# Gated recurrence in a two-block transformer kernel: cumulated decays made two rounds ahead, and the order of ScalarE and VectorE in a round

## The chip, the cores and the metric

The kernel runs on one core of a Trainium2 chip, as one launch. The metric is the device time of that launch in microseconds (us), the median of several runs. A profiled execution of the same program gives the rows shown below.

## The reference

The program computes two blocks one after the other, for one sequence of 256 positions and width 1024. The first block puts 16 meta tokens in front (272 positions), multiplies by one projection, and sends the parts to two mixers: a gated recurrence (HGRN2) with 8 heads of width 128, and a Mamba-2 mixer. Then come an output projection and a gated MLP with a short convolution. The second block has a retention mixer and 16 experts with expert choice. Only the HGRN2 mixer is touched by the change. Cut to what matters, per head:

```python
f = lb + (1.0 - lb) * sigmoid(f_pre)
k = 1.0 - f
log_f = log(f)
qa = silu(q)
bcum = cumsum(log_f)                       # restarted at every chunk of 16
q_dec, k_inv = q * exp(bcum), k * exp(-bcum)
k_end = k * exp(blast - bcum)
o = causal(q_dec @ k_inv.T) @ v + q_dec @ state
o = o * rsqrt(mean(o * o) + eps) * norm_w * silu(g)
```

`lb` is a vector with one number per channel, made from `hg_lb_logits`. The kernel uses the same recurrence at chunk lengths 16, 32, 64 and 128 (its four "levels").

## The kernel before, in words

All activations lie with channels on the partitions and the 272 positions along the row. The projection of the first block is made as 52 output tiles of 128 channels, numbered j = 0 to 51, in the order of `ORDER`. TensorE (PE) makes a tile with 8 products in fp32 (L872), in one of three PSUM banks that it uses in turn, so a tile can be opened only when the tile three before it has been copied out. ScalarE (ACT) copies each tile out (`evict`, L1254), with Silu, Sigmoid or a plain copy according to the block of columns. Every engine runs its instructions in the order in which they are written; the three loops `for j in range(NPROJ)`, one for each engine, set that order by hand, with semaphores between them.

From j = 32 on, the work of the HGRN2 heads is laid between the tiles, three steps (`hgrn(j)`) for one head h, so one round of a head takes three tiles:

- **Step 0.** PE `hg_turn(h)`: transposes of values and decayed keys (L793, L795), which wait for `hg_staged`; scores of the four levels (L802); then it waits for `hg_v` and makes the last small scores (L804), waits for `hg_ke` and makes the two states (L808). Then the tile j. ACT `hg_keys(h)` (L1373) copies the turned keys, `hg_log_mean(h-1)` takes Ln of the mean square of the head before (L1365), `hg_log(h+1)` takes Ln of the gate (L1351), `hg_inverse(h-1)` is an Exp (L1369), a Square of the output follows (L1390), then `hg_exps(h+1)` (L1356 to L1358), and only then the tile's copy. VectorE (DVE) has `hg_values(h)` (L1845, L1846; it signals `hg_v`), `hg_mask(h)` (L1853), `hg_states(h)` (L1860) and `hg_cumulate(h+1)`: gate (L1817), key (L1819), after `hg_log` four scans (L1822) and four differences (L1826).
- **Step 1.** PE `hg_out(h)` (L815 to L818) and tile j+1. DVE `hg_gate(h)` (L1867), `hg_finish(h-1)` (L1872), `hg_decay(h+1)` (L1835 to L1840; it signals `hg_staged`).
- **Step 2.** PE `hg_mean(h)` (L826) and tile j+2. For ACT only the tile's copy, for DVE nothing, apart from the last head.

Head 0 is prepared at j = 30. The heads' last steps fall behind the tiles, between the first products of the output projection (L890). At j = 48 and 49 a pass of the other mixer's gate lies in the same queues: DVE `m2_gate(0)` (L1800) and ACT `gate_squares(0)` (L1400). Before an activation whose function isn't in the loaded table, ACT has a table load, which the compiler puts in. Lines that say this best:

```python
pe.wait_ge(ev("hg_v"), h + 1)
pe.matmul(ps[0:16, 6, 384:400], hg_K0[:, b, 256:T], hg_B[:, b, 0, 256:T], start=True, stop=True).then_inc(ev("hg_scores"), 1)
...
evict(f"p{j}", proj[:, 4 * unit_ + m, :], T, fn)
```

Of the kernel before, what the change touches and what calls it, by code (L numbers as in the profile page):

```python
# [19 lines left out]
ACT = mybir.ActivationFunctionType  # L20
# [130 lines left out]
def build(nc, a, out):  # L151
    with ExitStack() as ctx:
# [106 lines left out]

        hg_f, hg_k, hg_lf, hg_sq = (proj[:, TBM + i, :] for i in range(4))  # L260

# [986 lines left out]
        def _(act):  # L1248
# [100 lines left out]
            def hg_log(h):  # L1349
                act.wait_ge(ev("hg_f"), h + 1)  # L1350
                act.activation(hg_lf, hg_f, ACT.Ln).then_inc(ev("hg_log"), 1)  # L1351

# [22 lines left out]
            def hgrn(j):  # L1375
# [3 lines left out]
                if (j - 32) % 3 == 0:  # L1379
                    hg_keys(h)  # L1380
                    if h:
                        hg_log_mean(h - 1)
                    if h + 1 < HEADS:
                        hg_log(h + 1)
                    if h:
# [4 lines left out]
                    act.activation(hg_sq, ps[:, 6, 0:T], ACT.Square).then_inc(ev("hg_squared"), 1)  # L1390
                    if h + 1 < HEADS:
                        hg_exps(h + 1)
                if (j - 32) % 3 == 2 and h == HEADS - 1:
                    hg_log_mean(h)
                    hg_inverse(h)

# [206 lines left out]
        def _(dve):  # L1603
# [33 lines left out]
            lb, oml = small[:, 96:104], small[:, 104:112]  # L1637
            st.link(tt(lb, small[:, 0:8], small[:, 24:32], ALU.mult))
            st.link(ts(oml, lb, -1.0, 1.0, ALU.mult, ALU.add))

# [173 lines left out]
            def hg_cumulate(h):  # L1814
                b = h % 2
                dve.wait_ge(ev("proj_tiles"), 16 if h < 4 else 32)
                st.link(ts(hg_f, proj[:, h + TF_, :], oml[:, h:h + 1], lb[:, h:h + 1], ALU.mult, ALU.add))  # L1817
                dve.nop().then_inc(ev("hg_f"), 1)
                st(ts(hg_k, hg_f, -1.0, 1.0, ALU.mult, ALU.add))  # L1819
                dve.wait_ge(ev("hg_log"), h + 1)  # L1820
# [53 lines left out]
            def hgrn(j):  # L1874
# [3 lines left out]
                if (j - 32) % 3 == 0:  # L1878
                    hg_values(h)
                    hg_mask(h)  # L1880
                    hg_states(h)
                    if h == 0:
                        mod_add(1)
                    if h + 1 < HEADS:
                        hg_cumulate(h + 1)
                if (j - 32) % 3 == 1:
                    hg_gate(h)
                    if h:
                        hg_finish(h - 1)
                    if h + 1 < HEADS:  # L1890
                        hg_decay(h + 1)
                if (j - 32) % 3 == 2 and h == HEADS - 1:
# [389 lines left out]
```

## Time and profile before

| | us |
|---|---|
| median of 3 runs (lowest, highest) | 1702.42 (1701.29, 1703.94) |
| the profiled execution, its own time | 1704.49 |
| its span, first to last instruction | 1702.7 |
| PE busy (share of the span) | 1349.4 (79%) |
| DVE busy | 507.1 (30%) |
| ACT busy | 450.4 (26%) |
| GpSimd busy | 232.8 (14%) |

The difference between a profiled execution's own time and its span lies around the program. A row of the timeline has start, duration, engine, line and operation, and in brackets how long the engine sat idle before it and what released it; "DVEq" is VectorE's own sequencer, which signals without an instruction that computes. PEld is TensorE's weight load, which runs beside its products. A line is that of the kernel before.

### The profile page before, as it was taken

To read this page: it belongs to the slowest core of one execution; us is meant where nothing else is said; L and a number is where in the kernel's file an instruction comes from. 1 tells how busy PE (TensorE), PEld (TensorE's weight loads), DVE (VectorE), ACT (ScalarE), POOL (GpSimd) and SP (SyncE) were. 2 spreads that over 40 slices of the span, in tenths; PEclk is the share of its full clock that TensorE was granted. 3 is DMA by queue.
4 is the path that set the end of the run, shared out by engine and by line. 5 is a ranking of instruction groups with operands and counts; after the bars stand their busy time and mean duration, and the time that the engine had idled before them with its cause. 6 is when DMAs were issued, how large, how long until landed. Compare 5 with 4: busy or idle time off the path is not lost.

```text
span 1702.7 us, 21054 instructions
## 1 busy us (share of the span) xinstructions
PE 1349.4 (79%) x8581; PEld 831.1 (49%) x8581; DVE 507.1 (30%) x919; ACT 450.4 (26%) x675; POOL 232.8 (14%) x100
## 2 busy tenths in 40 slices
PE   6989999999999999988767577666657667666665
PEld 4877788879998988944222122112212221221221
DVE  3874677436568455622000000000000000000001
ACT  4853465436564533721000000000000000000001
POOL 0000000028767654400000000000000000000000
PEclk9999999999999999997887878888887877987887
DMA  7936322168534552285999999999999999999995
GB/s 242 361 149 235 112 99 100 50 210 273 186 137 181 201 188 99 100 357 212 428 429 428 429 428 429 428 428 429 429 429 428 429 429 428 429 428 429 428 428 250
DMA packets 92335, 524.01 MB, mean 308 GB/s; under 512 B 8009, under 2 KB 30945, under 8 KB 64369
## 3 DMA queue, kind: packets, MB, share of 16 engines
q1 hardware_dynamic: 92057, 523.08, 75.4%
q8 instruction: 44, 0.72, 0.2%
q14 instruction: 18, 0.15, 0.0%
q10 hardware_dynamic: 216, 0.06, 0.0%
HBM read 522.08 MB, written 1.05 MB: 307 GB/s over the span
## 4 chain that ended last, share of the span: by engine, by line
DMA 47%; PE 38%; DVE 8%; ACT 3%; issue 1%; SPq 1%; POOL 0%; ACTq 0%; DVEq 0%
DMA ring<-in_w_down 23%; DMA ring<-in_w_up 23%; PE ps L657 6%; PE ps L661 6%; PE ps L658 6%; PE ps L1213 3%; PE ps L890 3%; PE ps L1226 3%; PE ps L872 2%; PE ps L1123 2%; PE ps L641 1%; SPq L502 1%; DVE arena L2024 1%; PE ps L802 1%; PE ps L706 1%
## 5 line engine op out<-in xcount | busy, mean ns | idle before, releaser
L1213 PE MATMUL ps<-ring,arena 128*32 128x512 f32 x1984 | 297.5, 745 | 163.2 <-DMA ring<-in_w_up 136.0
L1599 POOL TENSOR_TENSOR ring_r<-ring,ring_r 128x1024 fp32r<-128x1024 f32 (+1 forms) x96 | 232.6, 2441 | 483.3 <-ACT ring_r L1265 483.3
L657 PE MATMUL ps<-arena_r,ring_r 128*128 128x258 f32 (+3 forms) x960 | 289.3, 301 | 9.7 <-PE ps L661 3.4
L661 PE MATMUL ps<-arena_r,ring_r 128*128 128x258 f32 (+3 forms) x960 | 281.4, 293 | 0.0
L1226 PE MATMUL ps<-ring,arena 128*32 128x512 f32 x1024 | 171.2, 804 | 104.1 <-DMA ring<-in_w_down 97.1
L1213 PEld LDWEIGHTS ps<-ring,arena 128*32 128x32 f32 x1984 | 65.0, 127 | 378.3 <-DMA ring<-in_w_up 204.7
L657 PEld LDWEIGHTS ps<-arena_r,ring_r 128*128 128x128 f32 x960 | 183.2, 191 | 20.6 <-issue 13.2
L661 PEld LDWEIGHTS ps<-arena_r,ring_r 128*128 128x128 f32 x960 | 182.4, 190 | 2.9
L658 PE MATMUL ps<-arena_r,ring_r 128*128 128x256 f32 (+2 forms) x608 | 180.8, 297 | 0.0
L2239 DVE TENSOR_TENSOR arena<-arena,ps 128x512 f32<-128x512 f32 x16 | 11.0, 688 | 448.7 <-PE ps L1213 448.7
L1226 PEld LDWEIGHTS ps<-ring,arena 128*32 128x32 f32 x1024 | 33.0, 129 | 225.1 <-DMA ring<-in_w_down 147.6
L1265 ACT ACTIVATE ring_r<-ring 128x1024 fp32r<-128x1024 f32 (+1 forms) x122 | 126.0, 1037 | 42.9 <-PE ps L658 23.0
L658 PEld LDWEIGHTS ps<-arena_r,ring_r 128*128 128x128 f32 x608 | 116.3, 191 | 4.0 <-issue 1.0
L872 PE MATMUL ps<-uT,ring 128*128 128x272 f32 x416 | 100.2, 395 | 3.2 <-DVE uT L1643 3.2
L658 PE MATMUL ps<-uT_r,ring_r 128*128 128x258 f32 x352 | 99.5, 283 | 0.0
L2241 DVE COPY arena<-ps 128x512 f32<-128x512 f32 x16 | 11.1, 692 | 290.7 <-PE ps L1226 290.7
L1569 ACT ACTIVATE arena<-ps 128x512 f32<-128x512 f32 x16 | 9.6, 597 | 316.1 <-PE ps L1218 316.1
L872 PEld LDWEIGHTS ps<-uT,ring 128*128 128x128 f32 x416 | 77.6, 190 | 18.5 <-issue 3.6
L1567 ACT ACTIVATE arena<-ps 128x512 f32<-128x512 f32 x16 | 9.6, 597 | 282.7 <-PE ps L1213 282.7
L1573 ACT ACTIVATE arena<-ps 128x512 f32<-128x512 f32 x16 | 9.6, 597 | 264.6 <-PE ps L1226 264.6
L1235 PE MATMUL ps<-arena 128*128 128x512 f32 x128 | 67.1, 672 | 14.2 <-DVEq L2248 13.5
L641 PEld LDWEIGHTS ps<-arena,hT 128*128 128x128 f32 x512 | 65.8, 205 | 8.9 <-issue 7.1
(370 smaller groups left out, 1478.1 us busy)
## 6 DMA issues: line engine op xcount, KB each, us to landing
ring<-in_w_gate SPq DMA_DIRECT2D x64, 2048.0 KB, 25.9
ring<-in_w_down SPq DMA_DIRECT2D x64, 2048.0 KB, 26.2
ring<-in_w_up SPq DMA_DIRECT2D x60, 2048.0 KB, 21.9
ring<-in_w_in SPq DMA_DIRECT2D x20, 2048.0 KB, 11.7
ring<-in_w_ada SPq DMA_DIRECT2D x12, 2048.0 KB, 8.5
ring<-in_ffn_w_up SPq DMA_DIRECT2D x22, 1024.0 KB, 7.9
ring<-in_w_out SPq DMA_DIRECT2D x6, 2048.0 KB, 8.0
ring<-in_ffn_w_down SPq DMA_DIRECT2D x4, 2048.0 KB, 8.4
```

The source lines that it names most:

```text
L641: mm = pe.matmul(o, l, r, start=i == 0, stop=i == len(pairs) - 1)
L657: pe.matmul(o, hi[:, k, :], r_(xhi(k0 + k)), start=first and k == 0, stop=False)
L658: mm = pe.matmul(o, hi[:, k, :], r_(xlo(k0 + k)), start=False, stop=False)
L661: mm = pe.matmul(o, lo[:, k, :], r_(xhi(k0 + k)), start=False, stop=last and k == nk - 1)
L872: mm = pe.matmul(o[:, 0:T], w[:, k, :], uT[:, k, :], start=k == 0, stop=k == KT - 1)
L890: mm = pe.matmul(o[:, 0:KEPT], kcols(u_out[cb][half], m)[:, i, :], x, start=first and n == 0, stop=last and n == len(blocks) - 1)
L1123: mm = pe.matmul(ps[:, 4 + 2 * w + cb, :], x[:, w * P:w * P + P], slot(u_out2[cb]).rearrange("p (k c) -> p k c", k=KT)[:, i, :], start=n = ...
L1213: mm = pe.matmul(ps[32 * j:32 * j + 32, half, :], xs[:, kt, :], wk[:, 512 * j:512 * j + 512], start=kt == 0, stop=kt == KT - 1)
L1226: mm = pe.matmul(ps[32 * j:32 * j + 32, half, :], heT[:, j, 32 * i:32 * i + 32], w[:, j, 512 * half:512 * half + 512], start=i == 0, stop= ...
L1235: mm = pe.matmul(ps[:, 4 + b, :], Gt[:, w * P:w * P + P], ye[:, half * 512:half * 512 + 512], start=first, stop=last, skip_group_check=True)
L1265: act.activation(r_(rounded(c)), chunks[c][1], ACT.Copy).then_inc(ev("w_hi"), 1)
L1599: pool.tensor_tensor(r_(w), w, f_(rounded(c)), ALU.subtract).then_inc(ev("w_lo"), 1)
```

## The change

The gate itself is no longer stored. ACT takes the logarithm straight from the sigmoid, Ln(oml * sigmoid + lb) with one scale and one bias per channel, and DVE makes the key in one instruction, (lb - 1) * sigmoid + (1 - lb), for which one small vector `noml` is made once. `hg_log` now waits for `hg_b` of the head before, or, for head 0, for the other mixer's last output. In the rounds, head 1 is prepared as before, in round 0. From head 2 on, `hg_cumulate(h+2)` stands in step 2 of round h on DVE, `hg_exps(h+1)` in step 0 of round h on ACT ahead of the Square, and `hg_decay(h+1)` in step 0 of round h on DVE, behind `hg_states(h)`. `hg_log_mean(h)` moves from step 0 of round h+1 to step 2 of round h, and `hg_log(h+2)` stands behind it.

```diff
--- before.py
+++ after.py
@@ -257,7 +257,7 @@
         hg_S = A.take(2, P)
         hg_inv = A.take(1, T)[:, 0]
 
-        hg_f, hg_k, hg_lf, hg_sq = (proj[:, TBM + i, :] for i in range(4))
+        hg_k, hg_lf, hg_sq = (proj[:, TBM + i, :] for i in range(1, 4))
 
         A = Arena(x_at)
         m2_t = A.take(2, T)
@@ -1347,8 +1347,12 @@
                     act.activation(buf, buf, ACT.Exp).then_inc(ev("m2_seg_exp"), 1)
 
             def hg_log(h):
-                act.wait_ge(ev("hg_f"), h + 1)
-                act.activation(hg_lf, hg_f, ACT.Ln).then_inc(ev("hg_log"), 1)
+                if h:
+                    act.wait_ge(ev("hg_b"), h)
+                else:
+                    act.wait_ge(ev("m2_out"), 8)
+                lb, oml = small[:, 96 + h:97 + h], small[:, 104 + h:105 + h]
+                act.activation(hg_lf, proj[:, h + TF_, :], ACT.Ln, scale=oml, bias=lb).then_inc(ev("hg_log"), 1)
 
             def hg_exps(h):
                 b = h % 2
@@ -1378,21 +1382,24 @@
                     return
                 if (j - 32) % 3 == 0:
                     hg_keys(h)
-                    if h:
-                        hg_log_mean(h - 1)
-                    if h + 1 < HEADS:
-                        hg_log(h + 1)
+                    if h == 0:
+                        hg_log(1)
+                    elif h + 1 < HEADS:
+                        hg_exps(h + 1)
                     if h:
                         hg_inverse(h - 1)
                     act.wait_ge(ev("hg_out"), h + 1)
                     if h:
                         act.wait_ge(ev("hg_mean"), h)
                     act.activation(hg_sq, ps[:, 6, 0:T], ACT.Square).then_inc(ev("hg_squared"), 1)
-                    if h + 1 < HEADS:
-                        hg_exps(h + 1)
-                if (j - 32) % 3 == 2 and h == HEADS - 1:
+                    if h == 0:
+                        hg_exps(1)
+                if (j - 32) % 3 == 2:
                     hg_log_mean(h)
-                    hg_inverse(h)
+                    if h + 2 < HEADS:
+                        hg_log(h + 2)
+                    if h == HEADS - 1:
+                        hg_inverse(h)
 
             def gate_squares(g):
                 act.wait_ge(ev("m2_gated"), g + 1)
@@ -1636,6 +1643,8 @@
             st.link(dve.reciprocal(small[:, 24:32], small[:, 16:24]))
             lb, oml = small[:, 96:104], small[:, 104:112]
             st.link(tt(lb, small[:, 0:8], small[:, 24:32], ALU.mult))
+            noml = small[:, 112:120]
+            st(ts(noml, lb, -1.0, None, ALU.add))
             st.link(ts(oml, lb, -1.0, 1.0, ALU.mult, ALU.add))
 
             def scaled(name, k, t0):
@@ -1814,9 +1823,7 @@
             def hg_cumulate(h):
                 b = h % 2
                 dve.wait_ge(ev("proj_tiles"), 16 if h < 4 else 32)
-                st.link(ts(hg_f, proj[:, h + TF_, :], oml[:, h:h + 1], lb[:, h:h + 1], ALU.mult, ALU.add))
-                dve.nop().then_inc(ev("hg_f"), 1)
-                st(ts(hg_k, hg_f, -1.0, 1.0, ALU.mult, ALU.add))
+                st(ts(hg_k, proj[:, h + TF_, :], noml[:, h:h + 1], oml[:, h:h + 1], ALU.mult, ALU.add))
                 dve.wait_ge(ev("hg_log"), h + 1)
                 for l in range(4):
                     st(dve.tensor_tensor_scan(hg_B[:, b, l, :], reset[:, l, :], hg_lf, 0.0, ALU.mult, ALU.add))
@@ -1881,14 +1888,18 @@
                     hg_states(h)
                     if h == 0:
                         mod_add(1)
-                    if h + 1 < HEADS:
-                        hg_cumulate(h + 1)
+                    if h == 0:
+                        hg_cumulate(1)
+                    elif h + 1 < HEADS:
+                        hg_decay(h + 1)
                 if (j - 32) % 3 == 1:
                     hg_gate(h)
                     if h:
                         hg_finish(h - 1)
-                    if h + 1 < HEADS:
-                        hg_decay(h + 1)
+                    else:
+                        hg_decay(1)
+                if (j - 32) % 3 == 2 and h + 2 < HEADS:
+                    hg_cumulate(h + 2)
                 if (j - 32) % 3 == 2 and h == HEADS - 1:
                     hg_finish(h)
```

PE's instructions and their order are the same in both. On ACT, one round of head 2 before, from the keys' copy to the copy of the first tile (the names in it: `s_tiles_freed` and `s_tiles_done` are the PSUM tiles, the others the events named above):

```order
L1373 ACTIVATE arena<-ps 128x256 [waits s_tiles_freed,s_hg_turned]
L1365 ACT_TABLE_LOAD [waits s_hg_head]
L1365 ACTIVATE arena<-ps,eps 128x272 [waits s_hg_mean]
L1351 ACTIVATE arena<-arena 128x272 [waits s_hg_f]
L1369 ACT_TABLE_LOAD
L1369 ACTIVATE arena<-arena 128x272 [waits s_hg_log_mean]
L1390 ACTIVATE arena<-ps 128x272 [waits s_hg_mean,s_hg_out]
L1356 ACTIVATE arena<-arena 128x272 [waits s_hg_b]
L1357 ACTIVATE arena<-arena 128x1024
L1358 ACTIVATE arena<-arena 128x1088 [waits s_act_steps]
L1254 ACTIVATE arena<-ps 128x272 [waits s_tiles_done]
```

Both logarithms stand here between two copies of tiles, in step 0. The round of head 2 in the changed kernel, whose lines are numbered otherwise: L1377 is the keys' copy, L1360 to L1362 the exponentials, L1373 the inverse, L1394 the Square, L1369 the logarithm of the mean, L1355 that of the gate.

```order
L1377 ACTIVATE arena<-ps 128x256 [waits s_tiles_freed,s_hg_turned]
L1360 ACT_TABLE_LOAD
L1360 ACTIVATE arena<-arena 128x272 [waits s_hg_b]
...
L1362 ACTIVATE arena<-arena 128x1088 [waits s_act_steps]
L1373 ACTIVATE arena<-arena 128x272 [waits s_hg_log_mean]
L1394 ACTIVATE arena<-ps 128x272 [waits s_hg_mean,s_hg_out]
...
L1254 ACTIVATE arena<-ps 128x272 [waits s_tiles_freed,s_tiles_done]
L1369 ACT_TABLE_LOAD [waits s_tiles_freed,s_hg_head]
L1369 ACTIVATE arena<-ps,eps 128x272 [waits s_hg_mean]
L1355 ACTIVATE arena<-arena,small 128x272 [waits s_hg_b]
L1254 ACT_TABLE_LOAD
L1254 ACTIVATE arena<-ps 128x272 [waits s_tiles_done]
```

The logarithms and their table load now stand behind the copy of tile j+1, ahead of the copy of tile j+2. On DVE, before, from the finish of one round to the values of the next:

```order
L1872 TENSOR_TENSOR arena<-arena 128x272 [waits s_hg_gated,s_hg_inverse]
L1835 COPY small<-arena 128x1 [waits s_hg_exp]
L1836 TENSOR_TENSOR arena<-arena 128x272
L1837 TENSOR_TENSOR arena<-arena 128x1024
L1840 TENSOR_TENSOR arena<-arena 128x1088 [waits s_proj_tiles,s_dve_steps]
L1845 COPY arena<-ps 128x256 [waits s_dve_steps,s_hg_turned]
L1846 COPY arena<-ps 16x128
```

The same stretch in the changed kernel (L1879 is the finish, L1826 the key, L1829 the scans, L1833 the differences, L1852 and L1853 the values):

```order
L1879 TENSOR_TENSOR arena<-arena 128x272 [waits s_hg_gated,s_hg_inverse]
L1826 TENSOR_SCALAR arena<-arena,small 128x272 [waits s_proj_tiles]
L1829 SCALAR_TENSOR_TENSOR arena<-cst,arena 128x272 [waits s_hg_log]
...
L1833 TENSOR_TENSOR arena<-arena 128x256 [waits s_dve_steps]
...
L1852 COPY arena<-ps 128x256 [waits s_dve_steps,s_hg_turned]
L1853 COPY arena<-ps 16x128
```

The products of `hg_decay` have left this place for the one behind the states, and the scans and differences of the head after next have taken it.

## Rows read from the trace of the kernel before

**Rows 1.** The page: the span, and the chain that ended last by engine.
```profile
span 1702.7 us, 21054 instructions
...
DMA 47%; PE 38%; DVE 8%; ACT 3%; issue 1%; SPq 1%; POOL 0%; ACTq 0%; DVEq 0%
```

**Rows 2.** Waits, 170 to 320 us: total us, times, the longest.
```profile
ACT arena L1351 <- DVEq L1818: 25.4, 8, 6.6
...
PE ps L793 <- DVEq L1841: 3.3, 4, 2.1
...
PE ps L808 <- ACT arena L1373: 1.0, 1, 1.0
```

**Rows 3.** Timeline of PE, 223 to 257 us: a round of head 3.
```profile
239.94 0.49 PE L793 MATMUL ps<-cst,arena 128*128 128x128 f32 x3
...
242.37 0.21 PE L804 MATMUL ps<-arena 128*16 128x16 f32 x2
...
243.06 3.83 PE L872 MATMUL ps<-uT,ring 128*128 128x272 f32 x16
...
248.06 3.91 PE L872 MATMUL ps<-uT,ring 128*128 128x272 f32 x16
251.81 0.62 PE L826 MATMUL ps<-arena,ones 128*128 128x272 f32 x2
...
256.40 0.52 PE L793 MATMUL ps<-cst,arena 128*128 128x128 f32 x3 [0.30 <-DVEq L1841]
```

**Rows 4.** Timeline of DVE, 220 to 245 us.
```profile
230.00 2.57 DVE L1822 TENSOR_TENSOR_SCAN arena<-cst,arena 128x272 f32<-128x272 f32 x4
232.61 1.43 DVE L1826 TENSOR_TENSOR arena<-arena 128x256 f32<-128x256 f32 x4
234.27 0.50 DVE L1867 SCALAR_TENSOR_TENSOR arena<-ps,par,arena 128x272 f32<-128x272 f32 x1 [0.22 <-DVE arena L1826]
...
240.69 0.42 DVE L1845 COPY arena<-ps 128x256 f32<-128x256 f32 x1 [1.04 <-PE ps L795]
241.03 0.27 DVE L1846 COPY arena<-ps 16x128 f32<-16x128 f32 x1
```

**Rows 5.** Timeline of ACT, 220 to 245 us.
```profile
224.56 1.28 ACT L1365 ACT_TABLE_LOAD   x1
225.85 0.49 ACT L1365 ACTIVATE arena<-ps,eps 128x272 f32<-128x272 f32 x1
...
240.14 0.40 ACT L1254 ACTIVATE arena<-ps 128x272 f32<-128x272 f32 x1 [1.31 <-PE ps L872]
```

**Rows 6.** Line L1430, an activation with scale and bias per channel.
```profile
L1430 ACT ACTIVATE arena<-arena,par x12: 612/616/618, 31.0 to 70.4; 128x272 f32<-128x272 f32 x12
```

**Rows 7.** Timeline of all engines, 160 to 215 us: from round 0 into round 1.
```profile
196.23 0.41 DVE L1817 TENSOR_SCALAR arena<-arena,small 128x272 f32<-128x272 f32 x1
...
197.20 2.57 DVE L1822 TENSOR_TENSOR_SCAN arena<-cst,arena 128x272 f32<-128x272 f32 x4
...
202.73 1.11 ACT L1358 ACTIVATE arena<-arena 128x1088 f32<-128x1088 f32 x1
...
205.16 0.91 ACT L1254 ACTIVATE arena<-ps 128x272 f32<-128x272 f32 x2
...
206.95 0.55 PE L793 MATMUL ps<-cst,arena 128*128 128x128 f32 x3 [0.65 <-DVEq L1841]
...
209.43 0.21 PE L804 MATMUL ps<-arena 128*16 128x16 f32 x2
```

**Rows 8.** The same view: the turn of head 0 and the tile behind it.
```profile
187.67 0.55 PE L793 MATMUL ps<-cst,arena 128*128 128x128 f32 x3 [2.12 <-DVEq L1841]
...
192.38 2.92 PE L872 MATMUL ps<-uT,ring 128*128 128x272 f32 x12
```

**Rows 9.** Busy time by engine and granted clock (PEclk) in two stretches.
```profile
core 0: us, PE busy (x) PEld busy (x) DVE busy (x) ACT busy (x) POOL busy (x), PEclk, DMA share, GB/s
...
190.00:192.00 2.00, 2.00 (x11) 1.74 (x10) 0.23 (x1) 0.16 (x1) 0.00 (x0) 0.50 1.05 396
291.00:293.00 2.00, 1.04 (x10) 0.82 (x9) 1.11 (x4) 1.86 (x7) 0.00 (x0) 1.00 0.00 0
```

## The prediction

> **What bounds the kernel now.** I read the page first, for the chain that ended last: transfers hold 47% of it, and PE 38% [rows 1]. The transfers belong to the experts at the end; the stage that the change touches, about 176 to 330 us, lies ahead of them, and there the chain runs through PE with pieces of DVE and ACT. What this stage loses or gains moves everything behind it, because the later weight loads are released by PE's progress. I therefore count a microsecond here as a microsecond at the end.
>
> The waits of the stage come next [rows 2]. ACT sits 25.4 us in front of Ln of the gate, but an idle ACT costs nothing by itself. What counts is PE: it waits 3.3 us in total for `hg_staged` (DVE, L1841), 2.1 of them in front of head 0, and once 1.0 us for the keys' copy. The timeline shows how little that leaves: the turns of heads 3 and 4 start at 239.94 and 256.40, a round of 16.46 us with 0.30 of waiting [rows 3]. PE is nearly full, so a shorter chain can give back only these few waits, while a longer chain costs in every round. The question is where the new order puts its longest chain against PE's round.
>
> **The change, part by part.**
>
> *The gate in one ScalarE instruction.* For heads 0 and 1 nothing is moved, only the gate's DVE instruction no longer stands ahead of ACT's Ln. Before, the gate starts at 196.23 and the scans at 197.20, 0.97 us [rows 7]. Now Ln runs long before, and DVE needs only the key with two operands per channel, 0.41 us like the gate's row. So the scans start 0.55 us earlier, for head 0 and for head 1. Both times PE was waiting for `hg_staged` (2.12 us [rows 8] and 0.65 us [rows 7]), so both are gained, unless the DVE of round 0 is held by another wait: 0.55 each, 0 to 0.6 as bounds. In the later rounds the key's row is off the path. The Ln itself gets dearer: with scale and bias per channel I take 0.62 us from L1430 [rows 6] for the 0.49 or less of a logarithm without the scale [rows 5]. The one `noml` instruction on 8 columns is under 0.1 us and I count it as nothing; it hides beside the table loads and products of the start.
>
> *The moved products of `hg_decay`.* They now run behind the states of round h, for head h+1, about 8 us ahead of the next turn. PE's waits for `hg_staged` go from round 1 on: 3.3 less the 2.1 of head 0 is 1.2 us at most. In the forecast this gain isn't added, because the next part takes its place.
>
> *The cumulated decays, now behind the mean.* This is the term that decides. In step 2 of round h the chain is: PE ends tile j+1 and makes the mean; ACT copies tile j+1, loads the Ln table, takes both logarithms; DVE scans and subtracts for head h+2; and only then DVE may run `hg_values(h+1)`, for which PE waits in front of L804. Step by step, from the end of tile j+1: copy 0.43 with its start [rows 5]; semaphore 0.1; table load 1.28 [rows 5]; Ln 0.49 and Ln 0.62, overlapping a little, 1.04; semaphore 0.05; scans and differences until DVE is free, 230.00 to 234.27, 4.27 [rows 4]; values, 240.69 to 241.30, 0.61 [rows 4]; signal to PE 0.13. That is 7.91 us. The other half of the circle is PE's: from L804 at 242.37 over tile, output and the next tile to its end at 248.06 + 3.91 = 251.97, 9.60 us [rows 3]. The round becomes 7.91 + 9.60 = 17.5 us instead of 16.46, so 1.05 us more in each. The mean isn't the late one: it starts at 251.81 and ends at 252.43 [rows 3], and the table load now stands behind the copy anyway.
>
> *The first such chain is longer.* `hg_exps(1)` still comes at the end of ACT's step 0 in round 0, so its last row ends at 202.73 + 1.11 = 203.84 [rows 7], 203.29 with the 0.55 gained. Then follow a table load for the tiles' function 1.28, two copies 0.91 [rows 7], the Ln table 1.28, both Ln 1.04, scans and differences 4.27, values and signal 0.74, small steps 0.17: L804 of head 1 at 213.0 instead of 209.43 [rows 7]. That is +3.55 us, with both early gains already in it. PE starts the turn at about 206.35 and then stands some 4 us in front of L804.
>
> *From head 1 to head 6* there are five rounds with a `hg_cumulate(h+2)` in them: 5 x 1.05 = +5.3 us. In round 6 PE loses 1.0 us before, in front of L808 [rows 2], because the keys' copy stood behind the squares of the other mixer; in the new order DVE's `m2_gate(0)` runs ahead of the scans and the squares end before the copy is wanted: -1.0. Rounds 6 and 7 have no scans, and the steps behind the tiles keep their slack.
>
> *ACT's table loads.* There are four more over the whole program. Those in the rounds' chain are counted above, the others lie where ACT waits for a tile. The Trainium skill (ScalarE: Activation LUTs, Table sets: the hidden batching unit) speaks against such a change: activations should be batched by set. The same page (What ACT_TABLE_LOAD costs) puts a switch at about 2.66 us, the load of 1283 ns and a drain of about 1380 ns; by that the seven loads in my chains would be some 9.7 us dearer, a total near +19. The trace doesn't agree with the drain: the load at 224.56 lasts 1.28 us and the Ln starts at 225.85, 0.01 us later [rows 5].
>
> *PE's clock.* After the 2.12 us wait of head 0 the granted clock falls to 0.50, that is 1.2 of 2.4 GHz [rows 9], and from the turn to the tile PE takes 4.71 us (187.67 to 192.38 [rows 8]) against 3.12 (239.94 to 243.06 [rows 3]): 1.6 us more. After the stall of 1.0 us in round 6 it stays at 1.00 [rows 9]. A stall of 4 us is nearer to the first, so I take +1.6 once, for head 1. The stalls of about 1.3 us in the five later rounds lie between the two rows: 0 to 1.6 us each, and I take 0.
>
> **Sum.** +3.55 + 5.3 - 1.0 + 1.6 = +9.4 us. The rows come from an execution of 1704.49 us (span 1702.7), 2.1 above the median of the runs, 1702.42. The difference is the same whichever it is added to; added to the median it gives **1711.8 us**, and a profile of the changed kernel should have a span near 1712.
>
> **The rivals.**
>
> 1. *The same wait without the clock.* PE's stall of 4 us comes behind the transposes and scores and the clock stays up, or the fall of head 0 goes with its shorter wait (1.6 instead of 2.1 us). Then 1702.4 + 7.8 = 1710.2. For it speaks that 1.0 us costs no clock, against it the 2.1 us that did. If both falls are missing it is 1708.6.
> 2. *The clock falls again and again.* Each stall of 1.3 us lies in the part of the round where PE has small products. Two falls more give 1715.0, five 1719.8.
> 3. *Faster: the scans fit in front of the turn.* If PE isn't held at L804, only the gains stay: 0.55 twice, up to 1.2 of the later waits, 1.0 in round 6, together 3.3: 1699.1. The point from which this decides is the chain of 7.91 us: PE alone comes from the end of tile j+1 back to L804 in about 6.5 us (mean, tile, turn up to L804: 251.97 to 258.5), so the chain would have to be 1.4 us shorter, and in round 0 nearly 4. Durations of rows don't leave that open; it would need a mistake of mine in the order.
> 4. *Nothing measurable.* The stalls come as said, but half as long, since the order of ACT or the start of the scans is better than I think: between -3.4 and +3.4 us, which is also about what a measurement of this kernel can tell from no change (0.2%).
>
> **How the numbers follow.** Forecast with one fall of the clock at head 1: 0.43; rival 1: 0.25; rival 2: 0.20; rival 3: 0.04; rival 4: 0.08. The first three are all slower by more than 0.2% (above 1705.8): 0.88; within 0.2%: rival 4 and a half of rival 3: 0.09 with rounding; faster by over 0.2%: 0.03, as even the full gain of rival 3 only just reaches it. The range takes in rival 1 with both falls missing and an error of 0.25 us in each of six chains at the low end (1708.6 - 1.5 = 1707), and two to three falls more at the high end (1717): 1707 to 1717.
>
> **What would show it.** In the profile of the changed kernel PE must have a wait in front of the last small scores (L804) in heads 1 to 6, released by the values of DVE: some 4 us at head 1, 1.1 to 1.5 at the others; the wait at L808 in round 6 gone; turns of heads 3 and 4 some 17.5 us apart; `hg_staged` no longer waited for except at head 0, where the wait is 1.6 us. ACT's wait for Ln of the gate (25.4 us) should vanish, with no profit. The granted clock behind head 1's stall shows the last term. I am wrong if DVE's values start on time in round 2, if PE's round stays at 16.4 us, or if the difference at the end of the stage is made up later in front of the experts.

## The result, and the profile after

The changed kernel takes 1715.44 us in the median of 5 runs (1711.17 to 1718.82) against 1702.42 before (also 5 runs, 1701.29 to 1703.94); the ratio is 1.0075, with an interval of 1.0056 to 1.0093. It is slower, by about 13 us in the medians; a ratio and its interval come from all runs of both kernels, and can lie some 0.1% off the ratio of the two medians. The forecast was 1711.8, with a range of 1707 to 1717. The profiled execution of the change took 1715.44 us with a span of 1713.7; the one of before had a span of 1702.7, so the two traces differ by 11.0 us, and it is these 11.0 that can be followed row by row. The other 2 us are that the profiled execution of before lay 2.1 us above its median. One execution in the whole study, of split_signal below, came out at 2989.7 us with a granted clock of 0.44, and no median or ratio has it in.

The page of the changed kernel, its first and fourth part, against [rows 1]:

```profile
span 1713.7 us, 21043 instructions
...
DMA 47%; PE 37%; DVE 9%; ACT 4%; issue 1%; SPq 1%; POOL 0%; ACTq 0%; DVEq 0%
```

PE's share of the chain has fallen by a point, and those of DVE and of ACT have each risen by one. The waits of the stage (170 to 330 us; engine, line <- releaser: total us, times, the longest) say where:

```profile
ACT arena L1394 <- PE ps L818: 36.2, 8, 6.9
DVE arena L1829 <- ACT arena L1355: 23.6, 6, 5.0
...
PE ps L804 <- DVEq L1855: 9.6, 6, 3.9
...
PE ps L793 <- DVEq L1848: 1.5, 1, 1.5
```

In [rows 2] ACT stood 25.4 us in front of the gate's logarithm. That wait has gone, and ACT stands 36.2 us in front of its squares instead: no profit. PE has lost its wait in front of L808 (1.0) and all waits for `hg_staged` (L793) but the one of head 0. In their place stands a new one, 9.6 us in front of the last small scores, L804, once in each of heads 1 to 6, released by DVE's values (now L1852, L1853). PE's timeline shows them (start, us, engine, line, in brackets the wait and its releaser):

```profile
187.06 0.55 PE L793 MATMUL ps<-cst,arena 128*128 128x128 f32 x3 [1.48 <-DVEq L1848]
...
189.54 0.21 PE L804 MATMUL ps<-arena 128*16 128x16 f32 x2
...
210.59 0.24 PE L804 MATMUL ps<-arena 128*16 128x16 f32 x2 [3.88 <-DVEq L1855]
...
217.98 0.46 PE L815 MATMUL ps<-arena 128*128 128x128 f32 x2
...
231.11 0.21 PE L804 MATMUL ps<-arena 128*16 128x16 f32 x2 [1.35 <-DVEq L1855]
...
248.52 0.21 PE L804 MATMUL ps<-arena 128*16 128x16 f32 x2 [0.81 <-DVEq L1855]
...
301.15 0.21 PE L804 MATMUL ps<-arena 128*16 128x16 f32 x2 [1.35 <-DVEq L1855]
...
318.64 0.49 PE L793 MATMUL ps<-cst,arena 128*128 128x128 f32 x3
```

From head 2 to head 3 PE needs 248.52 - 231.11 = 17.41 us; the round of [rows 3] took 16.5. The chain that holds it is on ACT and DVE. It is shown here where it ends in PE's L804 of head 2, at 231.11:

```profile
223.34 0.40 ACT L1254 ACTIVATE arena<-ps 128x272 f32<-128x272 f32 x1 [1.66 <-PE ps L872]
223.89 1.28 ACT L1369 ACT_TABLE_LOAD   x1 [0.16 <-ACT arena L1254]
225.19 0.49 ACT L1369 ACTIVATE arena<-ps,eps 128x272 f32<-128x272 f32 x1
225.57 0.60 ACT L1355 ACTIVATE arena<-arena,small 128x272 f32<-128x272 f32 x1
```

```profile
226.21 2.57 DVE L1829 TENSOR_TENSOR_SCAN arena<-cst,arena 128x272 f32<-128x272 f32 x4 [4.98 <-ACT arena L1355]
228.81 1.43 DVE L1833 TENSOR_TENSOR arena<-arena 128x256 f32<-128x256 f32 x4
230.39 0.42 DVE L1852 COPY arena<-ps 128x256 f32<-128x256 f32 x1
230.73 0.27 DVE L1853 COPY arena<-ps 16x128 f32<-16x128 f32 x1
```

Copy of tile, load of Ln's table, Ln of the mean (L1369), Ln of the gate (L1355), scans, differences, and only then the values for which PE waits: 223.34 to 231.11, 7.77 us. One round later it runs from 240.75 to 248.52, 7.77 us again. DVE itself stood idle for 4.98 us in front of the scans, with the values that PE wanted queued behind them.

Where the 11.0 us are, from the first start of a line in each trace:

| from, to | before | after | difference |
|---|---|---|---|
| start of the span to the turn of head 0 (L793) | 187.7 | 187.1 | -0.6 |
| turn of head 0 to the first L890 | 117.3 | 126.4 | +9.1 |
| first L890 to the first L940 | 63.5 | 63.5 | 0.0 |
| first L940 to the experts' first L1213 | 418.3 | 422.0 | +3.7 |
| L1213 to the end | 916.0 | 914.8 | -1.2 |

### The profile page after: what moved, and what is told of

Same layout as the page of the kernel before. It is cut to its first block, busy times and chain, and to the rows that moved or that the text cites. A ratio compares the mean times of both kernels' runs of the same rounds, so it can differ in the third digit from the quotient of the medians.

```text
span 1713.7 us, 21043 instructions
## 1 busy us (share of the span) xinstructions
PE 1351.8 (79%) x8581; PEld 831.5 (49%) x8581; DVE 509.6 (30%) x912; ACT 455.5 (27%) x679; POOL 232.2 (14%) x100
## 3 DMA queue, kind: packets, MB, share of 16 engines
HBM read 522.08 MB, written 1.05 MB: 305 GB/s over the span
## 4 chain that ended last, share of the span: by engine, by line
DMA 47%; PE 37%; DVE 9%; ACT 4%; issue 1%; SPq 1%; POOL 0%; ACTq 0%; DVEq 0%
DMA ring<-in_w_down 23%; DMA ring<-in_w_up 23%; PE ps L657 6%; PE ps L661 5%; PE ps L658 5%; PE ps L1213 3%; PE ps L872 3%; PE ps L890 3%; PE ps L1226 3%; PE ps L1123 2%; PE ps L641 1%; DVE arena L1829 1%; DVE arena L2035 1%; SPq L502 1%; DMA ring<-in_w_in 1%
## 5 line engine op out<-in xcount | busy, mean ns | idle before, releaser
L1213 PE MATMUL ps<-ring,arena 128*32 128x512 f32 x1984 | 297.8, 746 | 162.9 <-DMA ring<-in_w_up 135.2
L657 PE MATMUL ps<-arena_r,ring_r 128*128 128x258 f32 (+3 forms) x960 | 289.7, 302 | 10.6 <-PE ps L661 3.3
L1213 PEld LDWEIGHTS ps<-ring,arena 128*32 128x32 f32 x1984 | 65.1, 127 | 377.9 <-DMA ring<-in_w_up 204.8
L657 PEld LDWEIGHTS ps<-arena_r,ring_r 128*128 128x128 f32 x960 | 183.5, 191 | 21.7 <-issue 13.0
L1265 ACT ACTIVATE ring_r<-ring 128x1024 fp32r<-128x1024 f32 (+1 forms) x122 | 126.0, 1037 | 42.9 <-PE ps L658 23.0
L1235 PE MATMUL ps<-arena 128*128 128x512 f32 x128 | 65.1, 656 | 14.2 <-DVEq L2259 13.5
```

The costliest lines, as they stand in the source:

```text
L657: pe.matmul(o, hi[:, k, :], r_(xhi(k0 + k)), start=first and k == 0, stop=False)
L1213: mm = pe.matmul(ps[32 * j:32 * j + 32, half, :], xs[:, kt, :], wk[:, 512 * j:512 * j + 512], start=kt == 0, stop=kt == KT - 1)
L1235: mm = pe.matmul(ps[:, 4 + b, :], Gt[:, w * P:w * P + P], ye[:, half * 512:half * 512 + 512], start=first, stop=last, skip_group_check=True)
L1265: act.activation(r_(rounded(c)), chunks[c][1], ACT.Copy).then_inc(ev("w_hi"), 1)
```

## The experiments

Where nothing else is said, an experiment stands against the kernel before, run on the same chip: 1703.36 us in the median of 23 runs for gate_alone, log_ahead, ln_doubled and fill_scores, 1702.60 of 18 for the other four. Single runs scatter by up to some 8 to 10 us (the kernel before 1701.51 to 1709.64, gate_alone 1698.27 to 1708.37), so I take medians of a few runs as good to one or two; the stage itself (turn of head 0 to the first L890) repeats much better, 126.4 and 126.0 us in two traces of the change. I therefore read the stage first and the total second.

My theory was that of the prediction: the round is closed by the chain through the Ln of the next-but-one head, 5 x 1.05 us; the first such chain costs PE a stand of 4 us, and the clock falls behind it. Against it stood three others: that the gate's part costs something; that what counts is not the chain but the new place of the scans or of the products; and that the stage isn't what moves the end.

**gate_alone: the gate's part without the new order.** The kernel before with these hunks of the change alone (and the one that makes `noml`):

```diff
-                act.wait_ge(ev("hg_f"), h + 1)
-                act.activation(hg_lf, hg_f, ACT.Ln).then_inc(ev("hg_log"), 1)
+                if h:
+                    act.wait_ge(ev("hg_b"), h)
+                else:
+                    act.wait_ge(ev("m2_out"), 8)
+                lb, oml = small[:, 96 + h:97 + h], small[:, 104 + h:105 + h]
+                act.activation(hg_lf, proj[:, h + TF_, :], ACT.Ln, scale=oml, bias=lb).then_inc(ev("hg_log"), 1)
...
-                st.link(ts(hg_f, proj[:, h + TF_, :], oml[:, h:h + 1], lb[:, h:h + 1], ALU.mult, ALU.add))
-                dve.nop().then_inc(ev("hg_f"), 1)
-                st(ts(hg_k, hg_f, -1.0, 1.0, ALU.mult, ALU.add))
+                st(ts(hg_k, proj[:, h + TF_, :], noml[:, h:h + 1], oml[:, h:h + 1], ALU.mult, ALU.add))
```

> The kernel before with the gate's part of the change alone: Ln straight from the sigmoid with scale and bias, one instruction for the key, all places in the rounds as before. Theory: the scans of heads 0 and 1 start 0.55 us earlier and PE waits that much less in front of both turns, and, as in the trace of the change, the clock may stay at 1.00 behind the turn of head 0, worth 1.6 us: 1.1 to 2.7 us under the kernel before, 1699.7 to 1701.3; in the other rounds up to 1.2 us more of waits for hg_staged vanish. Rival: the loss of the change lies in the dearer Ln (0.60 us instead of 0.43): then this kernel is slower than before by 0.17 us a head, 1.4 us.

Measured: 1701.36 us (1698.27 to 1708.37, 12 runs), ratio 0.9989 (0.9974 to 1.0005). The median is 2.0 us under that of the kernel before, though the interval of the ratio still takes in 1. The stage takes 114.0 us, 3.2 less than before. PE's waits in it that answer to [rows 2]:

```profile
PE ps L793 <- DVEq L1845: 1.5, 1, 1.5
...
PE ps L808 <- ACT arena L1377: 0.3, 1, 0.3
```

The 3.3 us of waits for `hg_staged` have become 1.5, all in front of head 0, and the one for the keys' copy 0.3 instead of 1.0. The 3.2 us add up: 1.2 of waits behind head 0, 0.7 at the keys, and 1.3 of clock behind the turn of head 0 (2.48 us from L793 to L804 instead of 3.82). So the gate's part alone already removes every wait that the products' new place was to remove: after it the order had only the 0.3 us at the keys left to gain in this stage. The rival that the dearer Ln of the gate's part makes the loss (+1.4 us, a ratio of 1.0008) is out.

**order_only: the new order without the gate's part.** The changed kernel with the old `hg_log` and the old gate and key in `hg_cumulate`, the hunks above turned round.

> The changed kernel's order with the gate as before: gate and key in two DVE instructions, Ln without scale and bias. Theory: the whole loss is in the order. The chain in front of L804 is 0.17 us shorter a round (Ln 0.43 instead of 0.60), six rounds -1.0 us; the scans of heads 0 and 1 start 0.55 us later, +1.1, and the clock may fall at head 0 as in the kernel before, +1.6: 0 to 1.7 us over the change, 1715.4 to 1717. PE waits in front of L804 at heads 1 to 6. Rival (the dear Ln with scale and bias makes the loss): back near the kernel before.

Measured: 1716.67 us (1713.58 to 1719.6, 6 runs), ratio 1.0070 (1.0055 to 1.0086); stage 127.4 us. Its waits:

```profile
PE ps L804 <- DVEq L1851: 8.5, 6, 3.7
...
PE ps L793 <- DVEq L1844: 2.8, 2, 2.1
```

The whole loss is the order's. The waits at L804 are 3.70, 1.17, 0.63, 0.68, 1.18 and 1.17 us, each 0.17 to 0.19 under those of the change, and the old Ln without scale takes 0.42 us on average, the new one 0.60: the same 0.18. So the dearer Ln of the gate's part, which costs nothing in the old order, is on the path in the new one. The turn of head 0 has its 2.1 us wait back. The total is 1.0 us over the change on the same chip (1715.64, change_again2 below), inside the 0 to 1.7 that were expected.

**log_ahead: the logarithm out of step 2.** The change, but ACT makes the gate's Ln of head h+2 in step 0 of the round, where the Ln's operand is long there:

```diff
                     elif h + 1 < HEADS:
+                        if h + 2 < HEADS:
+                            hg_log(h + 2)
                         hg_exps(h + 1)
...
                     if h == 0:
                         hg_exps(1)
+                        hg_log(2)
...
                     hg_log_mean(h)
-                    if h + 2 < HEADS:
-                        hg_log(h + 2)
```

> The changed kernel with hg_log(h+2) moved out of step 2 into step 0 of round h (in front of the exponentials; in round 0 behind them), so DVE's scans don't wait for ACT. Theory (the chain copy, Ln table, two Ln, scans, differences, values holds PE in front of L804): the waits of PE in front of L804 at heads 2 to 6 (5.7 us together in the change) are gone, though ACT has more table loads, 82 in all instead of 77; at head 1 DVE itself comes late, because hg_decay(1) ends just ahead of the turn and the scans and differences take 4.1 us: a wait of about 2.7 us stays there instead of 3.9. So 6.9 us under the change, about 1708.5, and up to 3 us less again if the clock doesn't fall at head 1. Rival (table loads on ACT, or DVE's own load, make the loss): no gain, or slower than the change by 5 x 1.28 us.

Measured: 1708.3 us (1704.63 to 1711.73, 12 runs), ratio 1.0024 (1.0013 to 1.0035); stage 117.8 us against 126.4. It comes within 0.2 us of what was expected, and in the place that was expected:

```profile
209.61 0.24 PE L804 MATMUL ps<-arena 128*16 128x16 f32 x2 [2.72 <-DVEq L1856]
...
215.73 0.46 PE L815 MATMUL ps<-arena 128*128 128x128 f32 x2
...
227.43 0.22 PE L804 MATMUL ps<-arena 128*16 128x16 f32 x2
```

Only the wait of head 1 is left, 2.72 us; from head 2 on PE never stands at L804 and the rounds are back at 16.0 to 16.5 us. The scans still stand in step 2 and the products behind the states, so from head 2 on neither of these two moves costs by itself: what closed the round was the Ln behind the mean. At head 1 it is otherwise. The Ln is there in time, and DVE is late all the same, because the scans of head 2 stand between the products for head 1 and the values. With the clock behind it (6.12 us from L804 to L815, 4.68 before) this stand is what keeps the stage 3.8 us above the 114.0 of gate_alone. So of the 12.3 us that the new order costs the stage, 8.5 go with the place of the Ln; the other 3.8 the trace puts down to the place of the scans ahead of head 1's values, which no run took away by itself.

**ln_doubled: the suspected link made dearer.** The change with the gate's Ln of step 2 made twice in six rounds.

```diff
                     if h + 2 < HEADS:
+                        lb, oml = small[:, 98 + h:99 + h], small[:, 106 + h:107 + h]
+                        act.wait_ge(ev("hg_b"), h + 2)
+                        st.link(act.activation(hg_lf, proj[:, h + 2 + TF_, :], ACT.Ln, scale=oml, bias=lb))
                         hg_log(h + 2)
```

> The changed kernel with Ln of the gate done twice over for heads 2 to 7, the second behind the first (0.60 us and some 0.1 us of semaphore each). Theory: this lies in the chain that holds PE, so each of six rounds is 0.7 us longer: 4.2 us over the change, about 1719.6, and PE's waits in front of L804 are that much longer. Rival (the chain is hidden, PE or the clock sets the rounds): no difference.

Measured: 1720.31 us (1718.72 to 1727.51, 5 runs), ratio 1.0090 (1.0070 to 1.0110).

```profile
PE ps L804 <- DVEq L1858: 13.5, 6, 4.5
```

Six more logarithms of 0.6 us add 13.5 - 9.6 = 3.9 us of PE's waits, 0.65 each: the Ln is on the path in all six heads, one for one. The stage grew by 8.7 us and not by 3.9, because in this trace the granted clock fell in three later rounds too; in 238 to 242 us its mean was 0.57. They are the rounds of heads 2, 5 and 6, where PE now stands 2.00 us and L804 to L815 takes 6.0 to 6.3 us instead of 4.4 to 4.7; behind the stands of 1.46 and 1.51 us of heads 3 and 4 it takes 4.37 as ever. The profiled execution was the highest of five (1727.51) and began the stage 4.9 us late; the median lies nearer to the expectation, 1719.6. Whether the other runs had these falls of the clock, no trace shows.

**fill_scores: is it the clock behind head 1?** The change with the scores of head 1 (L802) made three times, so that PE works in the time in which it would stand.

```diff
-                for l in range(4):
+                for l in list(range(4)) * (3 if h == 1 else 1):
```

> The changed kernel in which PE repeats the scores of head 1 twice more, 3.7 us of the 3.9 us that it stands in front of L804 there, with the same results. Theory (the clock falls because PE stands): the granted clock stays at 1.00 behind it, the stretch from L804 to the output's first product, 7.4 us in the change, goes to 4.4 us, so 3.0 us under the change, about 1712.4. Rival (the clock's fall has another cause, or the products cost more than the stall hides): no gain.

Measured: 1719.02 us (1713.7 to 1720.72, 6 runs), ratio 1.0078 (1.0058 to 1.0099). The total is a miss: I had forecast 1712.4. In the stage it did what was expected:

```profile
209.60 5.52 PE L802 MATMUL ps<-arena 128*128 128x128 f32 x48
215.44 0.21 PE L804 MATMUL ps<-arena 128*16 128x16 f32 x2 [0.31 <-DVEq L1855]
...
220.12 0.46 PE L815 MATMUL ps<-arena 128*128 128x128 f32 x2
```

Stretches around L804 of head 1, while PE would stand and behind it, first of this experiment, then of the change (us, then busy us and count of PE, PEld, DVE, ACT, POOL, then granted clock, DMA share, GB/s):

```profile
212.00:214.00 2.00, 2.00 (x20) 2.00 (x20) 1.97 (x5) 1.87 (x3) 0.00 (x0) 1.00 0.00 0
...
216.00:218.00 2.00, 2.00 (x12) 1.69 (x11) 1.83 (x6) 1.47 (x3) 0.00 (x0) 1.00 0.00 0
```

```profile
208.00:210.00 2.00, 0.00 (x0) 0.00 (x0) 1.82 (x6) 1.35 (x2) 0.00 (x0) 0.86 0.00 0
...
212.00:214.00 2.00, 2.00 (x5) 1.47 (x5) 1.72 (x7) 0.66 (x2) 0.00 (x0) 0.50 0.00 0
214.00:216.00 2.00, 2.00 (x6) 1.49 (x5) 1.97 (x3) 0.00 (x0) 0.00 (x0) 0.50 0.00 0
```

With PE kept at work the clock stays at 1.00 (2.4 GHz) and from L804 to L815 it takes 220.12 - 215.44 = 4.68 us; in the change it falls to 0.50 (1.2 GHz) while PE stands, stays there until a little after 216 us, and the same work takes 217.98 - 210.59 = 7.39, which is 2.7 more. The stage becomes 123.7 us, 2.7 less. Its profiled execution began the stage 4.8 us later (turn of head 0 at 191.90) and took 423.8 us from L940 to the experts; the six runs lie at 1713.7 to 1713.8 (two) and 1718.8 to 1720.7 (four). The slower four lie about as far above the other two as this late start is long, so the miss may sit ahead of the stage; no trace of one of the two shows it. That the clock behind head 1 costs 2.7 us of the stage is shown. That the end gets them back is not.

**change_again2: the change once more,** unaltered, to see what of its trace repeats.

> The changed kernel once more, beside the others on the same chip. Theory: PE's waits in front of L804 come again to 0.1 us (3.9 us at head 1, 0.8 to 1.4 at heads 2 to 6), so the first product of the output projection starts 8 to 9 us later than before. Behind that stretch the first profile of the change was 3.8 us longer up to the experts (418.3 against 422.0 us). If that belongs to the change, it is there again; if it is chance, this profile shows another value between 418 and 424.

Measured: 1715.64 us (1713.67 to 1718.84, 6 runs), ratio 1.0071 (1.0055 to 1.0087); the waits at L804 are again 3.88, 1.35, 0.81, 0.86, 1.35 and 1.36, and L940 to L1213 again 422.0. So the 3.7 us behind the stage were no accident of one execution.

**split_signal: a better kernel?** gate_alone, with ACT's signal for the decay products in two: K0 and D may be multiplied while ACT still makes its last exponential.

```diff
                 st.link(act.activation(hg_D[:, b], hg_D[:, b], ACT.Exp))
+                act.nop().then_inc(ev("hg_exp_d"), 1)
...
-                dve.wait_ge(ev("hg_exp"), h + 1)
-                st(dve.tensor_copy(small[:, 120 + b:121 + b], hg_B[:, b, 3, 255:256]))
+                dve.wait_ge(ev("hg_exp_d"), h + 1)
                 st(tt(hg_K0[:, b], hg_K0[:, b], hg_k, ALU.mult))
...
+                dve.wait_ge(ev("hg_exp"), h + 1)
+                st(dve.tensor_copy(small[:, 120 + b:121 + b], hg_B[:, b, 3, 255:256]))
```

> gate_alone with the exponentials' signal in two: DVE starts the products of keys and decays when ACT has made those two, while ACT still makes the third exponential (1.1 us). Theory: only the wait of PE for hg_staged at head 0 (1.5 us there) is on the path, so it shrinks by 1.0 us and nothing else moves: 1.0 us under gate_alone, about 1700.4. Rival: the semaphore of one more signal on ACT eats it: no difference.

Measured: 1702.49 us in the median of 11 runs (1698.04 to 1704.09), ratio 0.9989 (0.9978 to 1.0000). The total is a miss: about 1700.4 was expected, 1.0 under gate_alone, and the ratio is the same as that of gate_alone. PE's wait before head 0 is down from 1.48 to 0.38 us as meant:

```profile
PE ps L793 <- DVEq L1846: 0.4, 1, 0.4
```

The stage, 113.4 us, is the shortest of all, 0.7 under gate_alone, but its profiled execution took 422.0 us from L940 to the experts, like the change, although it has the old order. Together with gate_alone it suggests that the gate's half of the change is worth some 2 us in 1700 (0.9989 twice), at the limit of what can be measured. No version of this study beats the kernel before by more.

**busy_longer: does a microsecond of the stage reach the end?** gate_alone with the scores of heads 2 to 6 made twice: PE is busy and never stands. If later work absorbed what the stage loses, it would show here.

```diff
-                for l in range(4):
+                for l in list(range(4)) * (2 if 2 <= h <= 6 else 1):
```

> gate_alone in which PE repeats the scores of heads 2 to 6 once, with the same results: 5 x 1.9 us more of busy PE and no standing. Theory A (a microsecond of this stretch is one at the end, and only that): 9.4 us over gate_alone, about 1710.8, no fall of the clock in the rounds, and the stretch from there to the experts as long as in gate_alone (419 us). Theory B (a shift alone also lengthens what comes later, by where POOL and DVE then meet): that stretch is some 2 to 4 us longer, as it was in the four kernels with the new order, and the total 1713 to 1715.

Measured: 1710.94 us (1708.1 to 1715.76, 7 runs), ratio 1.0044 (1.0028 to 1.0061). That is 9.6 us over gate_alone, with 8.5 more in the stage (122.5 against 114.0), and theory A had 9.4. What the stage loses comes out at the end, all of it as nearly as these medians tell. From L940 to the experts it took 420.5 us against 419.1 in gate_alone. That lies between the two theories; the clock accounts for it (below).

**What the 3.7 us between L940 and the experts are.** They arise at two places, and both are of one kind: a DVE operation and one of GpSimd become ready almost together. At the first, DVE's row of the change, then GpSimd's:

```profile
473.30 2.62 DVE L1986 TENSOR_TENSOR arena_r<-arena,arena_r 128x256 fp32r<-128x256 f32 x1
```

```profile
473.05 5.10 POOL L1606 TENSOR_TENSOR ring_r<-ring,ring_r 128x1024 fp32r<-128x1024 f32 x2 [4.26 <-ACT ring_r L1265]
```

The same two in the kernel before:

```profile
464.87 0.42 DVE L1975 TENSOR_TENSOR arena_r<-arena,arena_r 128x256 fp32r<-128x256 f32 x1
```

```profile
464.97 4.94 POOL L1599 TENSOR_TENSOR ring_r<-ring,ring_r 128x1024 fp32r<-128x1024 f32 x2 [4.46 <-ACT ring_r L1265]
```

Before, DVE is 0.10 us ahead and takes 0.42 us; after, GpSimd is 0.25 us ahead and DVE takes 2.62. DVE stays late from there, and a product soon behind it (L657 at 479.20) waits 1.50 us for DVE, where the kernel before has no wait. From L940 to the last L986 behind this place it is 110.45 us before and 112.52 after, +2.1. GpSimd is first here in eight of the ten traces of this study, gate_alone, split_signal and busy_longer among them; only before and order_only have DVE first. At the second place, the change first:

```profile
724.00 2.81 DVE L2098 TENSOR_TENSOR arena<-arena,cst 128x512 f32<-128x512 f32 x1
```

```profile
723.87 2.39 POOL L1606 TENSOR_TENSOR ring_r<-ring,ring_r 128x1024 fp32r<-128x1024 f32 x1 [0.70 <-ACT ring_r L1265]
```

```profile
728.34 1.06 PE L1091 MATMUL ps<-cst,hT 128*128 128x128 f32 x8 [1.89 <-DVEq L2106]
```

The same three in the kernel before:

```profile
713.35 0.69 DVE L2087 TENSOR_TENSOR arena<-arena,cst 128x512 f32<-128x512 f32 x1
```

```profile
713.51 2.79 POOL L1599 TENSOR_TENSOR ring_r<-ring,ring_r 128x1024 fp32r<-128x1024 f32 x1 [0.98 <-ACT ring_r L1265]
```

```profile
715.92 1.03 PE L1091 MATMUL ps<-cst,hT 128*128 128x128 f32 x8
```

Before, DVE is 0.16 us ahead, takes 0.69 us, and PE doesn't wait. After, GpSimd is 0.13 us ahead, DVE takes 2.81 us, until 0.55 us behind GpSimd's end, and PE stands 1.89 us. All ten traces fall in line: with before, gate_alone and busy_longer DVE starts first, by 0.16 us each time, and takes 0.69; with the seven others GpSimd starts first, by 0.11 to 0.14 us, and DVE takes 2.80 to 2.82. From L940 to this L1091 it is 347.47 us before and 351.42 after, so both meetings together make +3.95, and what is left up to the experts is -0.2. The Trainium skill (SBUF — State Buffer, SBUF: two separate sides) says that a DVE operation with two inputs in SBUF and a GpSimd one that reads SBUF share a pair of ports under an exclusive lock, which the one that starts first keeps for its whole instruction. The ten traces agree with it at both places. Split_signal has the order of before and both meetings as in the change, so it isn't the new order as such that turns them round; between before and the change the two engines' starts moved against each other by 0.35 us at the first and 0.29 at the second. That a shift alone turns them round was not tried by itself.

Between the two meetings lies one more step of this size, in which the change and the kernel before agree. PE stands 1.80 to 1.84 us there for GpSimd in all ten traces; in seven of them, before and change too, the granted clock then falls to 0.50, and in gate_alone, log_ahead and ln_doubled it stays at 1.00. The stretch is 1.4 us shorter in these three. The change behind its stand of 1.81 us, then gate_alone behind its stand of 1.84 (columns as above; the granted clock is the third from the end):

```profile
560.00:565.00 5.00, 5.00 (x32) 5.00 (x31) 4.62 (x2) 1.63 (x2) 5.00 (x3) 0.66 0.99 401
```

```profile
548.00:553.00 5.00, 5.00 (x45) 5.00 (x44) 4.55 (x2) 1.55 (x2) 5.00 (x3) 1.00 0.99 397
```

That is why gate_alone, with the first meeting as in the change, still took only 419.1 us, and busy_longer 1.4 more.

## Why the prediction was right, and where it wasn't

The sign, the place and the mechanism were as predicted: PE waits at L804 in heads 1 to 6 for DVE's values, the wait at L808 is gone, `hg_staged` is waited for before head 0 alone, ACT's 25.4 us have gone without profit. Rivals 3 and 4 are out. (Rival 3's gains of 3.3 were too high in themselves: the 0.65 us wait of head 1 is in the second 0.55 and again in the 1.2.) That the measured 1715.44 lies in the range owes something to luck: the range reached up to 1717 for falls of the clock that did not come, and what filled it was not in the prediction (below). Term by term:

- **The rounds, 5 x 1.05.** Right. Chain 7.91 us forecast from the end of the tile; 7.82 measured (219.38 + 3.91 = 223.29 to 231.11). The three small gaps in it, 0.1, 0.05 and 0.13, for which the prediction has no row, are 0.15, 0.04 and 0.11 here. The rounds from head 2 to head 6 are 17.41, 17.42, 17.41 and 17.80 us against 17.5. The Ln with scale and bias takes 0.60 us where I took 0.62 from [rows 6]. From L804 of head 1 to that of head 6 it is 90.56 us, before 82.22 (209.43 to 291.65): +8.34. Of this 2.7 to 3.0 is the clock (below); 5.3 to 5.6 is left for five rounds. log_ahead shows that it is this chain, by taking it away.
- **Head 1, +3.55.** The step that was mis-sized: L804 of head 1 is at 210.59, only 1.16 us later than before [rows 7]. The wait itself, 3.88, is what I said (some 4), and the chain behind the last exponential is too: 201.05 to 210.59 is 9.54 us, against 9.7 in my working. But it began 2.8 us sooner (the exponentials' last row at 199.94 instead of 202.73), where I had counted 0.55. The 2.8 are 0.65 of the gate's own instruction, 0.61 from the turn of head 0, 1.34 from there to L804 (187.06 to 189.54, 2.48 us instead of 3.82, because the clock did not fall there) and 0.2 up to the values of DVE behind it. The sentence that +3.55 has "both early gains already in it" does not fit the working: 203.84 less 203.29 is one of them, and the earlier turn of head 0 is left out.
- **The clock, +1.6.** I had left head 0's fall in place and added one for head 1. What came was rival 1 at head 0 and my own case at head 1, dearer: the first fall vanished with the wait's shortening from 2.12 to 1.48 us, the second made 7.39 us from L804 to L815 out of 4.68 at the same head (4.36 in most other rounds), so 2.7 to 3.0 and not 1.6. I had taken the price of a short fall behind a 2.1 us stand for one behind a 3.9 us stand. Over the two, together with head 1's term, the two errors cancel in part: 1.16 + 3.0 = 4.2 where the sum had 3.55 + 1.6 = 5.2.
- **Round 6, -1.0.** Right: from L804 of head 6 to the turn of head 7 17.49 us, before 18.52 (291.65 to 310.17).
- **The stage's end.** +8.5 us at the turn of head 7 (318.64 against 310.17); the sum was +9.4.
- **"What moves here moves everything behind it"** holds in size (busy_longer) but I had taken it as exact. Behind the stage +3.7 and -1.2 us came on top, the +3.7 from the two meetings of DVE and GpSimd. Nothing in my sum asked what a shift of arrival does to near ties further on. So 1711.8 was 3.6 low although the stage came out 0.9 below the forecast: 2.5 came in behind the stage, and 2.1 because the sum was added to the median of before while its rows, and the 11.0 us followed here, are of an execution 2.1 above it.
- **Two early gains of 0.55.** Right for head 0 (0.64 of PE's wait). Their second effect, that a shorter wait there keeps the clock up, I had only in a rival.
- **The table loads.** In the round's chain the load lasts 1.28 us and Ln starts 0.02 later. The prediction's sum by the Trainium skill (ScalarE: Activation LUTs, What ACT_TABLE_LOAD costs), with about 1380 ns of drain behind each load, gave near +19; the traces don't agree with the drain, and the forecast without it was the right one.

Still open: the -1.2 us behind L1213; what decides, behind equal stands of 1.8 us, whether the clock falls; the end of fill_scores; and what makes the start of the stage come 5 us later in some executions (order_only, ln_doubled and fill_scores have their turn of head 0 at 191.9 to 192.7).

## What to carry to other kernels

Making something two rounds ahead doesn't help if the queue it is put into runs in order and the next thing that the busy engine wants stands behind it: ask of each moved step not when its own result is needed, but what is queued behind it and behind its wait. Here the early scans waited 5 us on DVE for an Ln, in front of two copies of 0.7 us in all for which PE stood. When a change has two halves, cost each against the waits of the kernel with the other half in: the gate's part alone had already emptied nearly all the waits that the order was made for.

## What was not expected of the hardware

- A stand of PE of 1.48 us in front of head 0 left the granted clock at 1.00 in the change, and in all seven traces that have it PE needed 2.5 us from there to L804; behind one of 2.12 and 2.13 us at the same place (before, order_only) the clock was at 0.50, and it needed 3.8 and 4.1. In ln_doubled PE's stands of 2.00 us cost clock and those of 1.46 and 1.51 did not. So in this stage a few tenths of waiting decided over another 1.3 to 1.7 us. But the length of the stand is not all of it: further on, equal stands of 1.80 to 1.84 us were followed by a fall in seven traces and by none in three. Behind the 3.88 us stand of the change the three stretches from 210 to 216 us are at 0.50; behind the 2.12 us stand of before it is the one from 190 to 192 alone, with 0.66 in the one ahead of it.
- The DVE operation on 128x512 takes 0.69 or 2.81 us by whether it starts 0.16 us ahead of GpSimd's or 0.13 us behind it, worth 1.9 us on PE; one on 128x256 takes 0.42 or 2.62 us in the same way, worth 2.1 us. Both turned round between before and the change.
